# A convolution's layer norm reduced to two numbers a row, with its sums, the last tile's copy and the second projection's first chunks reordered

## The chip, the cores and the metric

One Trainium2 chip, one core of it. The metric is the device time of one execution in microseconds (us), median of several runs; a profile is one further execution, recorded instruction by instruction. PE is TensorE, PEld its weight load, DVE VectorE, ACT ScalarE, POOL GpSimd, SP the queue that issues the DMAs.

## The reference, cut to what matters

Two blocks run one after the other on 256 rows of 2048 float32 channels. The change touches the second block's convolution layer alone:

```python
u = h @ w_pw1 + b_pw1                  # 2048 -> 4096
a, gate = jnp.split(u, 2, axis=-1)
u = a * jax.nn.sigmoid(gate)
u = depthwise_conv(u, w_dw) + b_dw     # 31 taps along the rows, each channel for itself
u = silu(layer_norm_2(u, ln_g, ln_b))  # over the 2048 channels, eps 1e-5
x = x + u @ w_pw2 + b_pw2              # the second projection
```

A gated MLP of width 8192 follows.

## The kernel before, in words

Activations lie channels on partitions: a tensor is 16 tiles of 128 channels by 256 rows. All weights stream once, as 686 chunks of 128x1024 float32 (512 KB) in a fixed order written by `plan` (line 45); `STEP[c]` is chunk c. For each chunk SP issues the load (L510) into one of 7 raw slots, ACT rounds it to a high part (`high`, L623, 4 slots), DVE (L971) or POOL (L566, for the chunks in `ON_POOL`) subtracts to a low part, and PE multiplies (L1693 and L1695, or L1698 to L1700 in the convolution's first projection). `s_mm` counts chunks that PE has finished; `high(c)` needs `s_mm >= c - 3`, the load of chunk c+6 needs `s_mm >= c`. Every engine runs its instructions in the order written, in one loop over c each, so whatever waits in a loop holds all that is behind it.

Chunks 328 to 394 are the first projection, tile by tile: "a" and then "gate" ("gt"). When a gate tile t is finished (chunk 348 for t=4, 361 for 7, 374 for 10, 387 for 13, 391 for 14, 395 for 15), ACT applies tanh (L743) and DVE writes the gated product (L1089, `s_pad`). Ten tiles are convolved on DVE with 31 taps each (`taps`, L1497), six a chunk. The other six, `ON_PE` = (4, 7, 10, 13, 14, 15), go to PE: SP writes the product to DRAM (L547), waits for that, and reads it back four times shifted (L550); PE then does a "cv" chunk of 64 small matmuls (L1800). These are chunks 356, 369, 382, 395, 396 and 397. SP does the copy of tile t after the load that its gate's end allows and the next one.

The layer norm. At `PIVOT` (chunk 384) PE sums tiles 0 to 7 over the channels with a matrix of ones (L1806), ACT copies the result (L957), and DVE subtracts that provisional mean from the tiles in five groups (`centre`, L1509), ACT squares them (`conv_squares`, L864). Tiles 0 to 7 are folded in pairs (L1626, L1629). After the last cv chunk `norm_conv` of each engine finishes: PE sums values and squares as full 128x256 products, ACT and DVE work out the reciprocal root as a 128x256 tile (L1517 to L1532), and DVE and ACT then normalise two tiles at a time: subtract the mean (L1525), multiply (L1539), SiLU (L878), rounding to the high part (L881), low part (L1542).

Chunks 398 to 429 are the second projection, 16 tiles of 2 chunks. The first four tiles are interleaved: the first halves of tiles 0 to 3 (398 to 401), then the second halves. A first half needs input tiles 0 to 7. A finished tile is added to the residual (L1093, L1096; `s_comb`) and starts the next norm (L754 to L1106).

At `POST` (end of the first block) the same kind of norm is already done with two numbers a row: sums against one column of ones (`stats`, L1730), a few operations on 128x2, `across` (L1414) to spread them on a diagonal, and a product with `unit` (L1883, L1886) that gives every partition the row. Chunks 328 to 335 already serve four products each (`together`, `chunk_for_all`).

Of the kernel before, what the change touches and what calls it, by code (L numbers as in the profile page):

```python
# [8 lines left out]
F32 = mybir.dt.float32  # L9
# [6 lines left out]
T = 256  # L16
# [28 lines left out]
def plan():  # L45
# [105 lines left out]
    group(*[Job("p2", t, "W", "w_p2", t, 2) for t in range(4)])  # L151
# [41 lines left out]
ON_POOL = {c for c in range(4, 32, 2)} | set(range(P1, P1_END + 4)) - PLAIN  # L193
# [44 lines left out]
def taps_plan():  # L238
# [26 lines left out]
    for c in range(P1, P1_END + 1):  # L265
# [21 lines left out]
LN2 = P1_END  # L287

# [6 lines left out]
def _build(nc, a, out, ctx):  # L295
# [101 lines left out]
    mA, m1, m2, rs = keep  # L397
# [17 lines left out]
    def row(ap):  # L415
# [50 lines left out]
    s_piv, s_mA, s_ctr, s_lsq, s_lnm, s_m1 = (sem("s_piv"), sem("s_mA"), sem("s_ctr"), sem("s_lsq"), sem("s_lnm"),  # L466
                                              sem("s_m1"))
# [37 lines left out]
    def sync(e):  # L505
# [17 lines left out]
        for c in range(1, NC + 1):  # L523
            if c + RAW - 1 < NC:
                w.wait_ge(s_mm, c)
                chunk(c + RAW - 1)
# [15 lines left out]

            j = ended(c - 1, "gt")
            if j is not None and j.t in ON_PE:
                i = ON_PE.index(j.t)
                w.wait_ge(s_pad, ON_PE[i] + 1)
                e.dma_start(a["padded"][i, :, :], wide[i]).then_inc(s_away, 16)  # L547
                w.wait_ge(s_away, 16 * (i + 1))
                for r in range(4):
                    e.dma_start(shifted[i][32 * r:32 * r + 32, :, :], a["padded"][i, :, :].rearrange(  # L550
                        "(g c) x -> c g x", g=4)[:, :, r:r + 284]).then_inc(s_shift[i % 3], 16)
# [5 lines left out]
    def gpsimd(e):  # L557
        w = Waits(e)

        def low(c):  # L560
# [53 lines left out]
    def scalar(e):  # L614
# [27 lines left out]
        def evac(j):  # L642
# [95 lines left out]
            elif j.stage == "gt":  # L738
# [4 lines left out]
                e.activation(kept(j), of(j), ACT.Tanh, scale=0.5, bias=hb[:, t:t + 1]).then_inc(s_evac, 1)  # L743
# [5 lines left out]
            elif j.stage == "p2":  # L749
# [3 lines left out]
                w.wait_ge(s_lnm, 2)  # L753
# [112 lines left out]
        def norm_conv():  # L866
            e.preload_act_table(ACT.Sqrt)
            for n in range(2, 5):
                conv_squares(n)
            w.wait_ge(s_lnm, 1)  # L870
            e.activation(m1, bank[7][:, 0:T], ACT.Copy).then_inc(s_m1, 1)
# [1128 lines left out]
```

## Time and profile before

| | us |
|---|---|
| median of three runs | 2104.72 |
| lowest and highest | 2104.37 and 2107.44 |
| the profiled execution, its own time | 2118.45 |
| its span in the trace | 2116.7 |
| PE busy in it | 2031.1 (96%) |
| DVE, ACT and POOL busy | 1619.4, 976.7 and 405.9 |

PE is busy nearly everywhere; the profile's forty slices are 52.9 us each and only three stretches show it waiting for long: the start, 1033 to 1044 us, and 1254 to 1293 us of the span, where the convolution's norm lies. The times named below are microseconds from the span's start.

### The profile page before, as it was taken

How to read it: one execution, taken by the hardware profiler on the slowest of the kernel's cores; microseconds unless marked ns; L12 is line 12 of the kernel's file. 1: busy time of each engine (PE TensorE's matmuls, PEld its weight loads, DVE VectorE, ACT ScalarE, POOL GpSimd, SP SyncE). 2: the span in 40 equal slices, each digit the busy share in tenths (PEclk: the TensorE clock that was granted, in tenths of full speed). 3: DMA queues.
4: the chain of work that ended last, by engine and by line, in shares of the span. 5: the costliest groups of instructions: out<-in, count | busy, mean ns of one | idle time of the engine just before them, and what ended most of it. 6: DMA issues, size and time to landing. Idle time of an engine off the chain costs nothing.

```text
span 2116.7 us, 30778 instructions
## 1 busy us (share of the span) xinstructions
PE 2031.1 (96%) x12116; PEld 1753.3 (83%) x12116; DVE 1619.4 (77%) x2528; ACT 976.7 (46%) x1438; POOL 405.9 (19%) x288
## 2 busy tenths in 40 slices
PE   7999999999899999999999988999999999999997
PEld 6787887788777788888899976888888888888886
DVE  8766889989899996688899957777567657656765
ACT  5544444444444445557543335544344434434442
POOL 3400233343233320000387750000000000000000
PEclk9999999999999999999999998999999999999998
DMA  7554554444544455565456553555555555555553
GB/s 292 200 182 160 189 181 158 145 164 150 168 150 159 151 183 184 184 225 188 140 182 209 180 181 109 189 188 183 187 189 184 186 188 188 184 185 189 186 184 118
DMA packets 106704, 378.01 MB, mean 179 GB/s; under 512 B 11968, under 2 KB 15808, under 8 KB 106560
## 3 DMA queue, kind: packets, MB, share of 16 engines
q1 hardware_dynamic: 106560, 376.04, 53.2%
q8 instruction: 96, 1.57, 0.3%
q14 instruction: 48, 0.39, 0.1%
HBM read 373.01 MB, written 2.98 MB: 178 GB/s over the span
## 4 chain that ended last, share of the span: by engine, by line
PE 73%; DVE 19%; ACT 3%; issue 3%; DMA 1%; POOL 0%; SPq 0%; DVEq 0%; ACTq 0%
PE bank L1693 38%; PE bank L1695 19%; DVE wl L971 6%; PE bank L1698 2%; PE bank L1699 2%; PE bank L1700 2%; ACT wh L623 2%; PE bank L1684 1%; PE bank L1682 1%; PE bank L1683 1%; DVE scr L1002 1%; PE bank L1800 1%; DVE sq L978 1%; DVE wsc L1286 1%; DVE wm L1276 1%
## 5 line engine op out<-in xcount | busy, mean ns | idle before, releaser
L971 DVE TENSOR_TENSOR wl<-raw,wh 128x1024 fp32r<-128x1024 f32 x598 | 748.5, 1256 | 346.5 <-ACT wh L623 345.4
L623 ACT ACTIVATE wh<-raw 128x1024 fp32r<-128x1024 f32 x680 | 710.6, 1054 | 539.7 <-PE bank L1695 384.3
L1693 PE MATMUL bank<-Hr,wh 128*128 128x512 f32 x2432 | 870.4, 402 | 17.6 <-DVE wl L971 12.4
L1693 PE MATMUL bank<-Yr,wh 128*128 128x512 f32 x2240 | 801.0, 402 | 27.0 <-DVE wl L971 10.9
L1695 PE MATMUL bank<-Hr,wl 128*128 128x256 f32 x2432 | 683.7, 281 | 0.0
L1695 PE MATMUL bank<-Yr,wl 128*128 128x256 f32 x2240 | 630.7, 282 | 0.0
L1693 PEld LDWEIGHTS bank<-Hr,wh 128*128 128x128 f32 x2432 | 458.9, 189 | 141.6 <-issue 12.8
L1693 PEld LDWEIGHTS bank<-Yr,wh 128*128 128x128 f32 x2240 | 423.8, 189 | 136.3 <-DVE wl L971 11.3
L1695 PEld LDWEIGHTS bank<-Hr,wl 128*128 128x128 f32 x2432 | 461.3, 190 | 0.3
L1695 PEld LDWEIGHTS bank<-Yr,wl 128*128 128x128 f32 x2240 | 426.1, 190 | 0.2
L566 POOL TENSOR_TENSOR wl<-raw,wh 128x1024 fp32r<-128x1024 f32 x82 | 203.1, 2483 | 399.7 <-ACT wh L623 399.7
L1698 PE MATMUL bank<-Hr,wh 128*128 128x256 f32 x448 | 127.5, 285 | 1.3 <-POOL wl L566 1.2
L581 POOL TENSOR_TENSOR wcs<-tab 128x256 f32<-128x256 f32 x32 | 38.8, 1214 | 461.2 <-DVE wm L1290 319.0
L1699 PE MATMUL bank<-Hr,wh 128*128 128x256 f32 x448 | 126.8, 283 | 0.0
L1700 PE MATMUL bank<-Hr,wl 128*128 128x256 f32 x448 | 126.7, 283 | 0.0
L1497 DVE SCALAR_TENSOR_TENSOR bank<-upad,cst,bank 128x256 f32<-128x256 f32 x290 | 121.7, 482 | 2.3
L767 ACT ACTIVATE Yr<-scrB 128x256 fp32r<-128x256 f32 x64 | 26.7, 418 | 146.3 <-DVE scrB L1114 146.3
L1698 PEld LDWEIGHTS bank<-Hr,wh 128*128 128x128 f32 x448 | 85.9, 192 | 3.1 <-issue 2.7
L1699 PEld LDWEIGHTS bank<-Hr,wh 128*128 128x128 f32 x448 | 86.0, 192 | 0.0
L1700 PEld LDWEIGHTS bank<-Hr,wl 128*128 128x128 f32 x448 | 86.0, 192 | 0.0
L688 ACT ACTIVATE scr<-scr 128x256 f32<-128x256 f32 x32 | 13.4, 418 | 115.3 <-DVE scr L1002 115.3
L1117 DVE TENSOR_TENSOR Yr<-scrB,Yr 128x256 fp32r<-128x256 f32 x64 | 27.2, 425 | 31.0 <-ACT Yr L767 31.0
(307 smaller groups left out, 1754.3 us busy)
## 6 DMA issues: line engine op xcount, KB each, us to landing
raw<-in_w_up SPq DMA_DIRECT2D x128, 512.0 KB, 3.2
raw<-in_w_dn SPq DMA_DIRECT2D x128, 512.0 KB, 3.2
raw<-in_w_g SPq DMA_DIRECT2D x96, 512.0 KB, 3.3
raw<-in_w_p SPq DMA_DIRECT2D x88, 512.0 KB, 4.2
raw<-in_w_b SPq DMA_DIRECT2D x48, 512.0 KB, 3.2
raw<-in_w_out SPq DMA_DIRECT2D x32, 512.0 KB, 3.2
raw<-in_w_bx SPq DMA_DIRECT2D x16, 512.0 KB, 4.5
raw<-in_w_q SPq DMA_DIRECT2D x16, 512.0 KB, 3.3
```

Source lines behind the costliest of these rows:

```text
L566: e.tensor_tensor(wl[:, c % RAW, :], raw[:, c % RAW, :], wh[:, c % WN, :].bitcast(F32), ALU.subtract).then_inc(s_low_g, 1)
L581: e.tensor_tensor(d[:, 0, :, :], *sides(0, 0), ALU.mult)
L623: e.activation(wh[:, c % WN, :], raw[:, c % RAW, :], ACT.Copy).then_inc(s_hi, 1)
L767: e.activation(hid.hi[:, t % 16, :], kept(j), ACT.Copy).then_inc(s_hidh, 1)
L971: e.tensor_tensor(wl[:, c % RAW, :], raw[:, c % RAW, :], wh[:, c % WN, :].bitcast(F32), ALU.subtract).then_inc(s_low_v, 1)
L1117: e.tensor_tensor(hid.lo[:, t % 16, :], s, hid.hi[:, t % 16, :].bitcast(F32), ALU.subtract).then_inc(s_hidl, 1)
L1497: e.scalar_tensor_tensor(ac, pad[:, j:j + T], wj, ac, ALU.mult, ALU.add).then_inc(s_v, w.own())
L1693: e.matmul(dst.rearrange("p (h t) -> p h t", h=2), lh, pair.both[:, :, k, :], start=first_part and kk == 0, stop=last_part and kk == 7, sk ...
L1695: ins = e.matmul(dst[:, 0:T], ll, pair.hi[:, k, :], start=False, stop=last_part and kk == 7, skip_group_check=True)
L1698: e.matmul(dst[:, 0:T], lh, pair.hi[:, k, :], start=first_part and kk == 0, stop=False)
L1699: e.matmul(dst[:, 0:T], lh, pair.lo[:, k, :], start=False, stop=False)
L1700: ins = e.matmul(dst[:, 0:T], ll, pair.hi[:, k, :], start=False, stop=last_part and kk == 7)
```

## The change

1. The second projection's first four tiles become one group (`together`): each of chunks 398 to 405 holds two input tiles' weights for four products, so chunk 398 needs input tiles 0 and 1 alone. A new weight array `w_p2g` holds them in this order. POOL makes the low parts up to chunk 405 (before: 401).
2. The pivot is taken over tiles 0 to 3 at chunk 367. Centring, squares and folds are spread over other chunks; the groups are (0-3), (4-7), (8-11), (12), (13,14), (15). Tiles 8 to 11 are added to the folds.
3. PE does all sums but those of tile 15 ahead of chunk 397, tile 15's convolution, and against one column (`stats`).
4. After tile 15 the mean and the reciprocal root are worked out on 128x2 and spread by one 128x512 product; values are multiplied and then the mean's share is subtracted, tile by tile for tiles 0 and 1, then in pairs. SiLU writes to PSUM.
5. The high parts of chunks 402 to 408 are made inside ACT's `norm_conv`, each after a pair of tiles.
6. SP does the copy of a tile ahead of the load of the chunk that its gate's end allows. The gates of tiles 14 and 15 stay in PSUM.

```diff
-    group(*[Job("p2", t, "W", "w_p2", t, 2) for t in range(4)])
+    together("p2g", "w_p2g", [Job("p2", t, "W", "w_p2", 0, 8) for t in range(4)], 1, 2)
-ON_POOL = {c for c in range(4, 32, 2)} | set(range(P1, P1_END + 4)) - PLAIN
+ON_POOL = {c for c in range(4, 32, 2)} | set(range(P1, P1_END + 8)) - PLAIN
-PIVOT = end("gt", 12) + 2
+PIVOT, NEXT = end("gt", 8) + 2, end("gt", 12) + 2
-CENTRED = ((0, 4), (4, 4), (8, 4), (12, 2), (14, 2))
+CENTRED = ((0, 4), (4, 4), (8, 4), (12, 1), (13, 2), (15, 1))
+NORMED = ((0, 1), (1, 1)) + tuple((t, 2) for t in range(2, 16, 2))
+NORMED_FOR = [next(n + 1 for n, (t, nt) in enumerate(NORMED) if t <= k < t + nt) for k in range(16)]
+HIGH_LN = range(LN2 + 4, LN2 + 11)
# sync
         for c in range(1, NC + 1):
+            j = ended(c, "gt")
+            if j is not None and j.t in ON_PE:
+                i = ON_PE.index(j.t)
+                w.wait_ge(s_pad, ON_PE[i] + 1)
+                e.dma_start(a["padded"][i, :, :], wide[i]).then_inc(s_away, 16)
+                w.wait_ge(s_away, 16 * (i + 1))
+                for r in range(4):
+                    e.dma_start(shifted[i]...)
             if c + RAW - 1 < NC:
                 w.wait_ge(s_mm, c)
                 chunk(c + RAW - 1)
-            j = ended(c - 1, "gt")
...
# gpsimd, low
+            if c >= P1_END + 3:
+                w.wait_ge(s_wide, 3)
# scalar
+                if t == 15:
+                    e.preload_act_table(ACT.Sqrt)
+                    conv_squares(2)
+                    conv_squares(3)
...
         def norm_conv():
+            conv_squares(5)
             w.wait_ge(s_lneps, 1)
+            e.activation(st[:, 10:12], st[:, 10:12], ACT.Sqrt).then_inc(s_lnroot, 1)
             e.preload_act_table(ACT.Silu)
+            for n, (t0, nt) in enumerate(NORMED):
+                val = bank[4 + n % 2][:, 0:nt * T].rearrange("p (n t) -> p n t", n=nt)
+                w.wait_ge(s_lns, n + 1)
+                if n >= 2:
+                    w.wait_ge(s_cpl, n - 1)
+                for t in range(t0, t0 + nt):
+                    e.activation(val[:, t - t0, :], Mf[:, t, :], ACT.Silu, ...)
+                w.wait_ge(s_lsil, t0 + nt)
+                e.activation(cp.hi[:, t0:t0 + nt, :], val, ACT.Copy).then_inc(s_cph, 1)
+                if LN2 + 2 + n in HIGH_LN:
+                    high(LN2 + 2 + n)
-            if len(ENDED.get(c, ())) > 1:
+            if c == end("gt", 1):
                 for j in ENDED[c]:
                     evac(j)
-            if c + 3 < NC and c + 3 not in HIGH_POST:
+            if c + 3 < NC and c + 3 not in HIGH_POST and c + 3 not in HIGH_LN:
                 high(c + 3)
-            if c in (PIVOT + 2, PIVOT + 3):
-                conv_squares(c - PIVOT - 2)
+            if c in (PIVOT + 2, NEXT + 1):
+                conv_squares(0 if c == PIVOT + 2 else 1)
+            if c == LN2 - 1:
+                conv_squares(4)
# vector, gate tile 15
+                if t == 15:
+                    taps("rest")
+                    centre(2)
+                    centre(3)
+                    w.wait_ge(s_ctr, 3)
+                    w.wait_ge(s_fold, 1)
+                    e.tensor_tensor(fold[0], fold[0], Mf[:, 8:12, :], ALU.add).then_inc(s_fold, 1)
+                    w.wait_ge(s_evac, j.evac)
+                e.scalar_tensor_tensor(pad[:, 15:271], of(j) if t >= 14 else kept(j), 1.0, ...)
+                if t == 15:
+                    w.wait_ge(s_lsq, 3)
+                    w.wait_ge(s_fold, 2)
+                    e.tensor_tensor(fold[1], fold[1], F1[:, 8:12, :], ALU.add).then_inc(s_fold, 1)
# vector, norm_conv
+            centre(5)
+            w.wait_ge(s_lnm, 1)
+            e.tensor_scalar(st[:, 14:18], bank[7][:, 0:4], 1.0, None, ALU.mult).then_inc(s_v, w.own())
+            e.tensor_tensor(mm, m, m, ALU.mult)
+            e.scalar_tensor_tensor(rs, sq, 1e-5, mm, ALU.add, ALU.subtract).then_inc(s_lneps, 1)
+            e.reciprocal(rs, rs)
+            e.tensor_tensor(mr, m, rs, ALU.mult)
+            e.tensor_tensor(dg, ident..., st[:, 10:14]..., ALU.mult).then_inc(s_dg, 1)
+            times(0)
+            for n, (t0, nt) in enumerate(NORMED):
+                f = Mf[:, t0:t0 + nt, :]
+                e.tensor_tensor(f, f, row(bank[6][:, T:2 * T]).broadcast_to((128, nt, T)), ALU.subtract)
+                if n + 1 < len(NORMED):
+                    times(n + 1)
+                if n >= 1:
+                    low_part(n - 1)
+            low_part(len(NORMED) - 1)
# vector, main loop
-            if c in (PIVOT + 1, PIVOT + 2):
-                centre(c - PIVOT - 1)
-            if c == PIVOT + 4:
+            if c in (PIVOT + 1, NEXT):
+                centre(0 if c == PIVOT + 1 else 1)
+            if c == LN2 - 1:
+                centre(4)
+            if c == NEXT + 2:
                 ... fold[0] of tiles 0 to 7
-            if c == PIVOT + 5:
+            if c == NEXT + 3:
                 ... fold[1]
# tensor
             if c == PIVOT:
-                conv_done(w, range(8))
-                sum_of(7, Mf, range(8), first_part=True, last_part=True).then_inc(s_piv, 1)
+                conv_done(w, range(4))
+                sum_of(7, Mf, range(4), first_part=True, last_part=True).then_inc(s_piv, 1)
+            if c == LN2 - 1:
+                sums_conv()
             if c == LN2:
                 norm_conv()
```

PE's `sums_conv` waits for the folds and then runs `stats` over fold[0] (4 tiles), fold[1] (4), tiles 12, 13 and 14 and their squares; its `norm_conv` runs `stats` over tile 15 and its squares, waits for `dg` and does the product `unit` by `dg`, 128x512.

## Rows read from the trace of the kernel before

**Rows 1.** The page's costliest groups: the three that make a chunk's two parts.

```profile
L971 DVE TENSOR_TENSOR wl<-raw,wh 128x1024 fp32r<-128x1024 f32 x598 | 748.5, 1256 | 346.5 <-ACT wh L623 345.4
L623 ACT ACTIVATE wh<-raw 128x1024 fp32r<-128x1024 f32 x680 | 710.6, 1054 | 539.7 <-PE bank L1695 384.3
L566 POOL TENSOR_TENSOR wl<-raw,wh 128x1024 fp32r<-128x1024 f32 x82 | 203.1, 2483 | 399.7 <-ACT wh L623 399.7
```

**Rows 2.** Table of stretches: PE, PEld, DVE, ACT, POOL busy, granted clock, DMA.

```profile
1254.40:1260.30 5.90, 0.05 (x6) 0.06 (x5) 0.78 (x1) 1.42 (x2) 2.57 (x2) 0.90 0.66 181
...
1262.00:1264.00 2.00, 2.00 (x24) 1.07 (x20) 0.00 (x0) 0.00 (x0) 0.00 (x0) 0.50 0.00 0
...
1289.00:1291.00 2.00, 1.74 (x6) 1.46 (x6) 1.97 (x3) 1.19 (x3) 0.00 (x0) 0.50 0.04 8
...
1295.00:1297.00 2.00, 2.00 (x13) 1.75 (x12) 1.02 (x2) 1.97 (x4) 0.00 (x0) 1.00 0.56 147
```

**Rows 3.** Timeline of PE (start, duration, instruction, idle before and releaser).

```profile
1210.09 3.62 PE L1806 MATMUL bank<-Mf,ones 128*128 128x256 f32 x16
...
1234.71 0.36 PE L1698 MATMUL bank<-Hr,wh 128*128 128x256 f32 x1 [0.85 <-POOL wl L566]
...
1247.30 7.11 PE L1800 MATMUL bank<-shifted,raw 128*32 128x256 f32 x128
1260.27 6.42 PE L1800 MATMUL bank<-shifted,raw 128*32 128x256 f32 x64 [5.85 <-DMA shifted<-padded]
...
1275.08 1.03 PE L1806 MATMUL bank<-F,ones 128*128 128x256 f32 x4
1283.21 0.77 PE L1693 MATMUL bank<-Yr,wh 128*128 128x512 f32 x1 [7.11 <-DVE Yr L1542]
...
1293.31 0.40 PE L1693 MATMUL bank<-Yr,wh 128*128 128x512 f32 x1
...
1293.66 0.39 PE L1693 MATMUL bank<-Yr,wh 128*128 128x512 f32 x1
```

**Rows 4.** Timeline of DVE from tile 12's product to the folds.

```profile
1208.56 2.55 DVE L1089 SCALAR_TENSOR_TENSOR upad<-scrB,scrB 128x256 f32<-128x256 f32 x1
...
1229.97 0.41 DVE L1089 SCALAR_TENSOR_TENSOR wide<-scrB,scrB 128x256 f32<-128x256 f32 x1
...
1234.37 1.27 DVE L1626 TENSOR_TENSOR fold<-Mf 128x1024 f32<-128x1024 f32 x1
1235.57 3.41 DVE L1629 TENSOR_TENSOR fold<-F 128x1024 f32<-128x1024 f32 x1
```

**Rows 5.** Timeline of SP's queue: tile 13's copy and the loads behind it.

```profile
1230.41 0.33 SPq L547 DMA_DIRECT2D padded<-wide  x1
1232.16 1.76 SPq L550 DMA_DIRECT2D shifted<-padded  x4
1233.96 1.38 SPq L510 DMA_DIRECT2D raw<-in_w_cv  x3
```

**Rows 6.** DMA view, 1190.3 to 1190.9: a load behind tile 10's copy, us to landing.

```profile
raw<-in_w_cv SPq DMA_DIRECT2D x1, 512.0 KB, 4.8
```

**Rows 7.** Timelines of ACT and DVE inside the norm.

```profile
1268.25 1.28 ACT L867 ACT_TABLE_LOAD   x1
...
1280.59 1.09 ACT L878 ACTIVATE Mf<-Mf,cst 128x256 f32<-128x256 f32 x2 [1.25 <-DVE Mf L1539]
1281.71 0.63 ACT L881 ACTIVATE Yr<-Mf 128x512 fp32r<-128x512 f32 x1
...
1282.37 0.69 DVE L1542 TENSOR_TENSOR Yr<-Mf,Yr 128x512 fp32r<-128x512 f32 x1
```

**Rows 8.** Timeline of PE at POST: sums against one column, and the spreading product.

```profile
1036.14 1.03 PE L1730 MATMUL bank<-ones,scrB 128*128 128x1 f32 x8
...
1040.02 1.19 PE L1883 MATMUL bank<-dg,unit 128*128 128x256 f32 x2 [1.31 <-DVE dg L1414]
```

**Rows 9.** Timeline of DVE: the second projection's first tile is added.

```profile
1305.51 0.48 DVE L1093 SCALAR_TENSOR_TENSOR Xf<-bank,cst,Xf 128x256 f32<-128x256 f32 x1
```

More of the change, by code:

```diff
@@ L263, in batch @@
                 return
-    for c in range(P1, P1_END + 1):
+    for c in range(P1, end("gt", 15)):
         for j in ENDED.get(c, ()):
@@ L396, in _build @@
     st = small[:, 32:64]
-    mA, m1, m2, rs = keep
+    mA = keep[0]
     def cv(name, i=0):
@@ L1511, in norm_conv @@
         def norm_conv():
-            taps("rest")
-            centre(2)
-            centre(3)
-            centre(4)
-            w.wait_ge(s_m1, 1)
-            e.tensor_tensor(m2, m1, m1, ALU.mult).then_inc(s_v, w.own())
-            n = w.n
-            def less(t0):
-                f = Mf[:, t0:t0 + 4, :]
-                w.wait_ge(s_ctr, 5)
-                w.wait_ge(s_lsq, 5)
-                w.wait_ge(s_fold, 1)
-                e.tensor_tensor(f, f, row(m1).broadcast_to((128, 4, T)), ALU.subtract).then_inc(s_v, w.own())
@@ L1527, in norm_conv @@
[L1527 to L1543 removed]
+            m, sq = st[:, 14:16], st[:, 16:18]
@@ new lines, in norm_conv, with times @@
+            w.wait_ge(s_v, w.n)
+            e.tensor_tensor(mr, m, rs, ALU.mult).then_inc(s_v, w.own())
+            w.wait_ge(s_v, w.n)
+            e.tensor_tensor(dg, ident[:, None, :].broadcast_to((128, 4, 128)),
+                            st[:, 10:14][:, :, None].broadcast_to((128, 4, 128)), ALU.mult).then_inc(s_dg, 1)
+            def times(n):
+                t0, nt = NORMED[n]
+                f = Mf[:, t0:t0 + nt, :]
+                w.wait_ge(s_wide, 3)
+                w.wait_ge(s_ctr, 6)
+                w.wait_ge(s_lsq, 6)
+                e.tensor_tensor(f, f, row(bank[6][:, 0:T]).broadcast_to((128, nt, T)),
+                                ALU.mult).then_inc(s_v, w.own())
@@ L1719, in chunk_for_all @@
                     a, z = k == 0 and j.col == 0, k == 15
+                    if j.kind == "W":
+                        both = bank[j.banks[0]]
+                        e.matmul(both.rearrange("p (h t) -> p h t", h=2), lh, pair.both[:, :, k, :], start=a, stop=z,
+                                 skip_group_check=True)
+                        ins = e.matmul(both[:, 0:T], ll, pair.hi[:, k, :], start=False, stop=z, skip_group_check=True)
+                        if z and j.tells:
+                            ins.then_inc(s_grp, 1)
+                        continue
                     e.matmul(of(j), lh, pair.hi[:, k, :], start=a, stop=False, skip_group_check=True)
@@ L1808, in sum_of, with sums_conv @@
             return ins
[L1810 to L1826 removed]
+        def sums_conv():
+            w.wait_ge(s_mA, 1)
+            w.wait_ge(s_fold, 4)
+            for t in range(4):
+                stats(fold[0][:, t, :], 0, first_part=t == 0)
+            for t in range(4):
+                stats(fold[1][:, t, :], 2)
+            w.wait_ge(s_ctr, 4)
+            stats(Mf[:, 12, :], 0)
+            w.wait_ge(s_lsq, 4)
+            stats(F1[:, 12, :], 2)
+            w.wait_ge(s_ctr, 5)
+            for t in (13, 14):
+                stats(Mf[:, t, :], 0)
+            w.wait_ge(s_lsq, 5)
+            for t in (13, 14):
+                stats(F1[:, t, :], 2)
+        def norm_conv():
+            w.wait_ge(s_ctr, 6)
+            stats(Mf[:, 15, :], 0)
+            w.wait_ge(s_lsq, 6)
+            stats(F1[:, 15, :], 2).then_inc(s_lnm, 1)
+            w.wait_ge(s_dg, 3)
+            e.matmul(bank[6], unit, dg, start=True, stop=True).then_inc(s_wide, 1)
         for c in range(NC):
```

103 lines of the change are left out of this document (37 added, 66 removed).

## Prediction

> **What bounds the kernel now.** I read the page first: PE is busy for 96% of the span, so time can only come from the stretches where it waits or runs at the lower of its two clocks, 1.2 and 2.4 GHz. The table of stretches then shows where: from 1254.4 to 1260.3 PE does nothing, after that the granted clock is 0.50 (1.2 GHz), and it is 0.50 again in the second projection's first chunks, where PE is busy 1.74 of 2 us [rows 2]. The timeline of PE gives the waits: 5.85 us for tile 15's copy, then tile 15's convolution in 6.42 us where two such chunks had taken 7.11 together, then sums until 1276.1, then 7.11 us in which DVE and ACT work out the norm [rows 3]. One sum over eight tiles, the pivot, stands in the middle of weight chunks (1210.1 to about 1213.4), and behind it PE waits 0.85 us for POOL's low part [rows 3]. Last I read what limits the helpers around chunk 387: DVE's timeline [rows 4] and SP's queue [rows 5].
>
> Two marks measure the change: E, the end of tile 15's convolution (1266.7 before [rows 3]), and N, the time at which chunk 406 can start. Before, PE reaches the higher clock at 1293.31 with 12 of the group's 64 weight tiles multiplied, and one takes 0.35 us (1293.31 to 1293.66) [rows 3]: 52 x 0.3475 = 18.1, so N = 1311.4, or E + 44.7. Behind N PE runs through in both kernels.
>
> **Part 1, from N backwards: the norm and the grouped chunks.** After E, ACT first makes chunk 401's high part (1.05, [rows 1]) and evacuates tile 15 (about 0.5); DVE's centring, no longer beside a POOL part, and the square take about 0.45 each (by the 0.48 of a tile-wide operation [rows 9]); the last four records of the sums half of 1.03 [rows 8]; with the handovers 3.3. At POST, PE stands 1.31 us between its last sum and the spreading product [rows 8]; here there are three more small operations (0.2 each, an estimate) and `dg` is twice as wide (+0.3): 2.2. The product has 512 columns for 256: 1.19 at the lower clock [rows 8], taken twice without its fixed part, 2.1 (at the higher clock about 1.2). So the row stands in PSUM at E + 7.6. Before, PE's first product of the projection began at 1283.2, E + 16.5 [rows 3].
>
> Of the normalisation DVE does six operations ahead of the first low part's end, four of them and the low part itself a tile wide and one two tiles (0.69 [rows 7]): 3.0. Chunk 398 needs just two tiles, 8 x 0.64 = 5.1 us at the lower clock, and ends at 8.2 after the row. Then the order on ACT decides: `high(402)` to `high(408)` each wait until PE has finished the chunk four before, and the next SiLU stands behind it. From the end of a chunk: high part 1.05 [rows 1], SiLU of two tiles 1.09, its high part 0.63, DVE's low part 0.69 [rows 7], handovers 0.15: 3.6, then the chunk that this feeds, 2.8: two chunks in 6.4, or 3.2 for one, where PE needs 2.8. Chunk 400 ends at 13.8, 402 at 20.1, 404 at 26.5, 405 at 29.3.
>
> A wait comes in behind it: chunk 406 writes the bank of the group's first product and needs `s_comb`. All four products end with chunk 405. DVE's loop does `low(409)` ahead of that evacuation, and ACT can't make its high part before chunk 405 is done: 1.05 + 1.26 [rows 1] + two operations of 0.48 [rows 9], 3.4 in all. The evacuations of the four (some 2.5 each) stand in front of `low(410)`; that is 14 us for which four chunks of 2.8 and the 3.4 are the cover: just enough. N = E + 7.6 + 29.3 + 3.4 = E + 40.3. **Part 1 gains 4.4.**
>
> **Part 2, up to E.** The pivot falls from 16 records to 8 (3.3 us, [rows 3]): -1.6. Its place, and `conv_squares` moved away from chunks 386 and 387, also take away the idle time behind it: 1213.4 to 1247.3 for eleven chunks of 2.88 leaves 2.2. So without a new wait chunk 393 would start at 1238.
>
> The new wait is SP's. Tile t's copy now stands ahead of the load of chunk e+6, where e is the chunk count at its gate's end. SP waits for the product, writes (1.75 until the next issue), issues four reads (1.8) [rows 5], and only then the load, which takes 4.8 beside them [rows 6]; ACT 1.05 and POOL 2.48 [rows 1] follow: 12.0 from the product to the chunk's readiness. PE wants it 6 x 2.88 = 17.3 after the gate's end. So the product must be there 5.3 after it. For tiles 4, 7 and 10 it is there after 3.9: cover 1.4, cost nothing on PE; but ACT stands 4 to 5 us in the high part of the waiting chunk, the next gate's tanh is some 2 us late, and DVE, full since chunk 367, keeps part of that.
>
> For tile 13 the product is late already before: it starts at 1229.97 [rows 4], 7.6 after the gate's end (1213.4 + 3 x 2.9 = 1222.3). Now: tile 12's product starts at about 1211.0 (1208.6 [rows 4], plus the first centring moved ahead of it, 2.6, and ACT's lateness, less the idle time that swallows a part). From it to tile 13's there were 21.4 us with two centrings of 2.65; now one, which POOL no longer blocks (1.2), and the first fold, moved ahead (1.27 alone, 3.4 beside POOL [rows 4]; I take 2.0): 21.4 - 5.3 + 3.2 = 19.3. It starts at 1230.3, and if POOL's low part comes first, as it did between the two folds, it is done at 1232.7; the ends are 1227 (nothing late at tile 11, fold at 1.2) and 1233. The gate's end is now at 1220.6. Chunk 393 is ready at 1232.7 + 12.0 = 1244.7 instead of 1238: **PE waits 6.7**, bounds 1 and 7.
>
> From there PE is full: chunks 393 and 394 2 x 2.88; the clock lost in the wait, 1.5 (bounds: 0, and 2.9 for one chunk at half rate); two convolution chunks 7.1 [rows 3]; the sums ahead of chunk 397, 56 records at 0.115 = 6.4 [rows 8], and 0.2 of waiting; tile 15's convolution 3.6 at the higher clock, since no idle time stands ahead of it: E = 1244.7 + 24.6 = 1269.3. Under the sums are hidden tile 15's copy (product at 1256.4, which itself waits for `high(398)` on ACT, then 7.1 for write and reads and landing to 1263.6, sums until 1265.7) and tile 14's centring. **Part 2 costs 2.6**; bounds -5.6 and +4.
>
> The squares of tiles 8 to 12 now follow a table load set behind tile 15's tanh. In the trace the load takes 1.28 and the next ACTIVATE starts 1.3 after it [rows 7]; squares, fold and sums start at 1259.6, just when PE is ready. By the Trainium skill (ScalarE: Activation LUTs, What ACT_TABLE_LOAD costs) a switch of set costs about 2.66 us with its drain. The trace doesn't agree; by the page E would be 1.4 later.
>
> **Sum.** +2.6 - 4.4 = -1.8, against the profiled execution's span of 2116.7 (own time 2118.45, 0.65% above the median; I carry the difference over as it is): 2104.72 - 1.8 = 2102.9. About 0.2% (4.2 us) is what a measurement can tell from no change.
>
> **Rivals.** (a) Chunk 393 waits little or not at all: the product comes before 1228, because DVE catches up or a late chunk delays PE and not DVE. Then E = 1238 + 23.1 = 1261.1, -5.6, and the whole is -10.0: 2094.7; with half the wait 2099. For it: PE has a large cover in every other copy. Against: DVE's own line leaves it no idle time from 1208 on [rows 4].
>
> (b) The grouped chunks stay at the lower clock: PE waits 0.4 in each 3.2, and before it was at 0.50 while busy 1.74 of 2 [rows 2]. Five more chunks at 5.1 for 3.2 would cost 9.5; but at 5.1 PE is busy throughout, as it was when it rose at 1293, so one or two chunks, 2 to 4 us: -1.8 + 4 = +2, 2107. By the Trainium skill (TensorE: Matmul & The Clock Gate, A second HAM failure mode) short idle times between groups of matmuls can make the clock go up and down.
>
> (c) Slower: the wait at chunk 393 drops the clock, and it stays at 1.2 GHz through 393, 394 and both convolution chunks, as it stayed over all of tile 15's (6.42 us at 0.50, [rows 2, 3]). That is 2.9 + 2.9 + 2.8 + 2.8 = 11.4 instead of 1.5: +9.9, 2112.8. It decides once three of the four are slow (+6 or more on -1.8). Against: weight chunks brought the clock back at 1293 within four microseconds of full work.
>
> (d) It does nothing: both halves hide behind the copy of tile 15. Then the time is 2104.7. Against: the 16.5 us after E lie in nobody's shade.
>
> **Chances.** Forecast 0.50 (own range 2099.5 to 2105.5), (a) 0.25, (b) 0.12, (c) 0.09, (d) 0.04. Faster than 2100.5: most of (a) and a quarter of the forecast, 0.36. Slower than 2108.9: (c) and a little of (b), 0.11. The rest 0.53. The range 2096 to 2108 leaves out the lower half of (a) and (c).
>
> **What would show it.** In the timeline of PE: the pivot with 8 records near 1159; a wait of about 6.7 us before chunk 393 near 1238, with the load issued about 1236 behind tile 13's reads; sums of 128x1 ahead of tile 15's convolution and that in 3.6 us; PE's first projection product 10 to 11 us after E; chunks 400 to 405 each 3.2 apart; a wait of some 3.4 us ahead of chunk 406 for DVE's L1096 operation. No wait at chunk 393 makes the forecast wrong toward (a); a clock of 0.50 behind it for over 6 us, toward (c).

## The result and the profile of the changed kernel

| | before | changed |
|---|---|---|
| median of nine runs, us | 2104.72 | 2113.36 |
| lowest and highest, us | 2103.35 and 2110.36 | 2110.08 and 2125.55 |
| the profiled execution, its own time | 2118.45 | 2117.75 |
| its span | 2116.7 | 2116.0 |

The ratio is 1.0039, 95% interval 1.0028 to 1.0051: about 8.2 us slower, clearly more than a measurement needs. Forecast were 2102.9 and a range of 2096 to 2108. The prediction was wrong, in its sign as well.

The two spans are nearly alike and must not be compared as wholes. PE ran through the second block's MLP in 100 us stretches of 568 records in the one profile and of 579 in the other, 2% apart, in a part that the change leaves alone; what causes it is not known. So I measure on PE between two marks that bracket the change: from the first product of the first projection to the product that starts the MLP's norm. From the timeline of PE, before and after:

```profile
1044.52 0.55 PE L1720 MATMUL bank<-Hr,wh 128*128 128x256 f32 x1 [1.75 <-issue]
...
1386.21 0.38 PE L1736 MATMUL bank<-keep,ones 128*128 128x256 f32 x1
```

```profile
1048.81 0.55 PE L1772 MATMUL bank<-Hr,wh 128*128 128x256 f32 x1 [1.75 <-issue]
...
1399.00 0.59 PE L1788 MATMUL bank<-keep,ones 128*128 128x256 f32 x2
```

That is 341.7 and 350.2: 8.5 us more, about what the medians say (8.6). The changed kernel's profile runs 4.3 us late from its first mark on, so 4.3 is to be taken from its times when they are set beside those of before.

The changed kernel's timeline of PE through the region answers to [rows 3] and [rows 8]:

```profile
1164.04 1.89 PE L1858 MATMUL bank<-Mf,ones 128*128 128x256 f32 x8
...
1248.65 0.55 PE L1742 MATMUL bank<-Hr,wh 128*128 128x256 f32 x1 [5.91 <-POOL wl L570]
...
1264.02 3.73 PE L1782 MATMUL bank<-ones,fold 128*128 128x1 f32 x32
1267.62 0.85 PE L1782 MATMUL bank<-ones,Mf 128*128 128x1 f32 x4
1268.33 0.99 PE L1782 MATMUL bank<-ones,F 128*128 128x1 f32 x4
1269.19 1.85 PE L1782 MATMUL bank<-ones,Mf 128*128 128x1 f32 x8
1270.89 1.84 PE L1782 MATMUL bank<-ones,F 128*128 128x1 f32 x8
1272.67 6.28 PE L1852 MATMUL bank<-shifted,raw 128*32 128x256 f32 x64
1281.01 0.66 PE L1782 MATMUL bank<-ones,Mf 128*128 128x1 f32 x4 [2.07 <-DVE Mf L1534]
...
1284.53 2.08 PE L1887 MATMUL bank<-dg,unit 128*128 128x512 f32 x2 [2.00 <-DVE dg L1552]
1289.33 0.77 PE L1766 MATMUL bank<-Yr,wh 128*128 128x512 f32 x1 [2.73 <-POOL wl L570]
...
1321.05 0.51 PE L1737 MATMUL bank<-Yr,wh 128*128 128x512 f32 x1 [3.31 <-DVE Xf L1121]
```

Four things are to be seen. The wait ahead of chunk 393 is there, 5.91 us. The one-column sums begin at 0.117 us a record (3.73 for 32) and end at 0.23 (1.84 for 8), with no idle time between. Tile 15's convolution, with no wait ahead of it, still takes 6.28. And the wait of 3.31 stands ahead of chunk 406. (The releaser at 1289.33 is misread: POOL's low part had begun at 1286.75 for a later chunk; DVE's first low part of the norm ended at 1289.24.)

The table of stretches of the changed kernel (columns as in [rows 2]) shows what the sums do to the granted clock:

```profile
1257.00:1264.00 7.00, 7.00 (x129) 4.04 (x128) 1.65 (x2) 5.35 (x7) 3.48 (x2) 1.00 0.57 200
1264.00:1267.60 3.60, 3.60 (x36) 3.58 (x33) 1.86 (x1) 1.42 (x2) 3.53 (x2) 1.00 1.03 291
1267.60:1272.70 5.10, 5.10 (x30) 5.08 (x30) 0.65 (x1) 0.63 (x1) 0.10 (x1) 0.52 0.35 142
1272.70:1279.00 6.30, 6.25 (x65) 2.77 (x64) 0.00 (x0) 0.00 (x0) 0.00 (x0) 0.58 0.00 0
...
1322.00:1326.00 4.00, 4.00 (x16) 3.38 (x15) 2.78 (x9) 1.43 (x4) 0.00 (x0) 0.57 0.00 0
```

PE's records are back to back from 1257 to 1279, yet the granted clock is 0.52 (1.2 GHz) from 1267.6 to 1272.7 and 0.58 from there to 1279. The load on the memory doesn't explain it: DMA was at 1.03 in the stretch with the clock at 1.00, and at 0.00 in the last of these with 0.58. The last line is the wait ahead of chunk 406 at work: behind it ten records run at the lower clock.

DVE's and SP's timelines of the changed kernel answer to [rows 4] and [rows 5]: the fold and the slowed product of tile 13, then the write, the reads, and only then the two weight loads.

```profile
1232.41 1.90 DVE L1666 TENSOR_TENSOR fold<-Mf 128x1024 f32<-128x1024 f32 x1
1234.23 2.62 DVE L1110 SCALAR_TENSOR_TENSOR wide<-scrB,scrB 128x256 f32<-128x256 f32 x1
```

```profile
1236.88 0.33 SPq L531 DMA_DIRECT2D padded<-wide  x1
1238.63 1.75 SPq L534 DMA_DIRECT2D shifted<-padded  x4
1240.43 0.91 SPq L513 DMA_DIRECT2D raw<-in_w_p  x2
```

### The profile page after: what moved, and what is told of

It is laid out like the page before. It is cut to its first block, busy times and chain, and to the rows that moved or that the text cites. A ratio compares the mean times of both kernels' runs of the same rounds, so it can differ in the third digit from the quotient of the medians.

```text
span 2116.0 us, 30837 instructions
## 1 busy us (share of the span) xinstructions
PE 2027.8 (96%) x12134; PEld 1756.1 (83%) x12134; DVE 1606.3 (76%) x2537; ACT 976.9 (46%) x1439; POOL 413.0 (20%) x292
## 4 chain that ended last, share of the span: by engine, by line
PE 69%; DVE 22%; issue 3%; ACT 3%; DMA 2%; SPq 1%; POOL 0%; ACTq 0%; DVEq 0%; POOLq 0%
PE bank L1737 38%; PE bank L1739 19%; DVE wl L983 7%; DVE bank L1522 2%; ACT wh L627 2%; PE bank L1726 1%; PE bank L1728 1%; PE bank L1727 1%; PE bank L1742 1%; PE bank L1743 1%; PE bank L1744 1%; DVE scr L1014 1%; PE bank L1852 1%; DMA raw<-in_w_p 1%; DVE wm L1301 1%
## 5 line engine op out<-in xcount | busy, mean ns | idle before, releaser
L1737 PE MATMUL bank<-Yr,wh 128*128 128x512 f32 x2176 | 770.4, 399 | 23.6 <-DVE wl L983 11.4
L1739 PE MATMUL bank<-Yr,wl 128*128 128x256 f32 x2176 | 609.0, 280 | 0.0
L1737 PEld LDWEIGHTS bank<-Yr,wh 128*128 128x128 f32 x2176 | 410.8, 189 | 125.4 <-DVE wl L983 11.8
L1739 PEld LDWEIGHTS bank<-Yr,wl 128*128 128x128 f32 x2176 | 412.0, 189 | 0.2
L570 POOL TENSOR_TENSOR wl<-raw,wh 128x1024 fp32r<-128x1024 f32 x86 | 213.0, 2486 | 424.3 <-ACT wh L627 405.2
```

The lines of the kernel that those rows point to most:

```text
L1737: e.matmul(dst.rearrange("p (h t) -> p h t", h=2), lh, pair.both[:, :, k, :], start=first_part and kk == 0, stop=last_part and kk == 7, sk ...
L1739: ins = e.matmul(dst[:, 0:T], ll, pair.hi[:, k, :], start=False, stop=last_part and kk == 7, skip_group_check=True)
```

## The experiments

The theory after reading the two traces has three costs: the wait at chunk 393; the clock that falls within the one-column sums and slows them and tile 15's convolution; the wait ahead of chunk 406 and the clock behind it. Each is tried alone against the changed kernel, then all together. "Ratio" is against the kernel before, "on PE" the time between the two marks (341.7 before, 350.2 changed). The second column scatters by some 1.5 us: the part behind chunk 406 took 77.9 us in some profiles and 76.6 in others with the same instructions, a weight tile every 0.353 us in the former and every 0.347 in the latter; the clock came back up to 2 us sooner or later in the group; and the wait at chunk 393 was anything from 5.45 to 7.09 us in the six profiles whose kernels leave the copies and the folds as the changed kernel has them.

| kernel | ratio (95% interval) | on PE |
|---|---|---|
| changed kernel | 1.0039 (1.0028 to 1.0051) | 350.2 |
| 1 all copies late | 1.0008 (0.9991 to 1.0024) | 342.8 |
| 2 two tiles' sums behind | 1.0018 (1.0007 to 1.0029) | 347.5 |
| 3 bank 7 | 1.0018 (1.0008 to 1.0029) | 349.7 |
| 4 wide products beside the sums | 1.0038 (1.0026 to 1.005) | 349.2 |
| 5 chunk 401's high part later | 1.0033 (1.001 to 1.0057) | 345.9 |
| 6 tile 13's copy alone late | 1.0031 (1.0013 to 1.0048) | 346.3 |
| 7 bank 7, evacuations spread | 1.0013 (0.9999 to 1.0027) | 345.9 |
| 8 all together | 0.9967 (0.9954 to 0.998) | 338.3 |
| 9 and tile 15's gate first | 0.9973 (0.9964 to 0.9982) | 336.1 |
| 10 folds behind tile 13's product | 1.0023 (1.0012 to 1.0034) | 344.4 |
| 11 as 9, with POOL's low parts | 0.9964 (0.995 to 0.9977) | 335.0 |
| 12 as 11, tile 15's copy early | 0.9953 (0.9934 to 0.9973) | 334.5 |

### 1. All copies where they were

```diff
-            j = ended(c, "gt")
-            if j is not None and j.t in ON_PE:
...
             if c + RAW - 1 < NC:
                 w.wait_ge(s_mm, c)
                 chunk(c + RAW - 1)
+            j = ended(c - 1, "gt")
+            if j is not None and j.t in ON_PE:
...
```

> SP does every tile's copy where the kernel before did it, behind the load of the next chunk; all else as in the changed kernel. Theory (the wait of 5.9 us at chunk 393 is the load held behind tile 13's copy, and the slow stretch behind it belongs to it; tile 15's copy keeps a cover of 8.7 us of sums): no wait at chunk 393, about 1.1 us less at the lower clock, tile 15's copy 1.4 us later but still covered: 7 us less than the changed kernel, 2106.4; the granted clock still falls in the one-column sums and tile 15's convolution still takes 6.3 us. Rival (the time is lost at tile 15 anyway): PE waits the same 6 us before tile 15's convolution and the time stays at 2113. Second rival (the wait at chunk 393 is what lowers the clock later): tile 15's convolution takes 3.6 us and the time is 2104 or less.

Measured: 6.5 us of the 8.2 come back by the ratios, 7.4 on PE. No wait at chunk 393; the clock falls in the sums all the same (0.95 from 1256 to 1260, 0.50 from 1260) and tile 15's convolution still runs mostly at the lower clock. So both rivals fall, and the wait at chunk 393, with the clock lost behind it, is the largest cost of the change. But the old order turns out to have a cost of its own. SP's timeline of this kernel, from tile 14's write on:

```profile
1242.35 0.33 SPq L534 DMA_DIRECT2D padded<-wide  x1
1247.82 1.75 SPq L537 DMA_DIRECT2D shifted<-padded  x4
1249.61 1.85 SPq L513 DMA_DIRECT2D raw<-in_w_p2g  x4
1251.51 0.93 SPq L534 DMA_DIRECT2D padded<-wide  x1
1260.81 1.75 SPq L537 DMA_DIRECT2D shifted<-padded  x4
```

Tile 14's write took 5.5 us until its reads could be issued and tile 15's 9.3, each behind four weight loads just issued; tile 13's, with no load just issued, 1.75. PE waits 1.84 for tile 14's reads here and 0.55 for tile 15's. Putting the copy ahead of the loads shortens the write; it only mustn't be done for a tile whose product is late.

### 2. The sums of tiles 13 and 14 behind tile 15's convolution

```diff
             stats(F1[:, 12, :], 2)
+
+        def norm_conv():
             w.wait_ge(s_ctr, 5)
             for t in (13, 14):
                 stats(Mf[:, t, :], 0)
             w.wait_ge(s_lsq, 5)
             for t in (13, 14):
                 stats(F1[:, t, :], 2)
-
-        def norm_conv():
             w.wait_ge(s_ctr, 6)
             stats(Mf[:, 15, :], 0)
```

> The sums of tiles 13 and 14 (16 records, 3.5 us at the lower clock) stand behind tile 15's convolution instead of ahead of it. Theory: tile 15's convolution starts 3.5 us earlier (about 1269.2), provided its reads have landed, and the sums then fill the 2.1 us in which PE waits for tile 15's centring, and stick out of it by 1.6 at the lower clock, 0 at the higher: 1.9 to 3.5 us less than the changed kernel, 2110 to 2111.5. The granted clock falls at the same point of the sums (1267.6), since 44 such records stand ahead of it. Rival (the copy of tile 15 lands only when the sums end): PE waits 3 us for the reads and nothing is gained, 2113 to 2115.

Measured: 2.7 on PE, 4.4 by the ratios (whose intervals overlap). The convolution followed the sums without a wait (its reads had landed), and took 6.12; so 40 one-column records ahead of it cost the clock as 56 did. Behind it the clock had risen, the 16 records took 2.0, and PE waited only 0.19 for tile 15's centring. A gain as forecast, from work that fits into a wait. From the timeline of PE:

```profile
1265.27 6.12 PE L1852 MATMUL bank<-shifted,raw 128*32 128x256 f32 x64
1271.31 1.05 PE L1782 MATMUL bank<-ones,Mf 128*128 128x1 f32 x8
```

### 3. Chunk 406 in a free bank

```diff
+        if t == 4:
+            j = jobs[-1]
+            held[j.banks[0]] = j.before[0]
+            b, j.banks, j.before = j.banks[0], [7], []
```

> The fifth tile of the second projection (chunks 406 and 407) goes to bank 7, which is free, instead of bank 0, which waits for the group's first evacuation. Theory: the wait of 3.3 us ahead of chunk 406 goes and with it the 1.8 us at the lower clock behind it: 5.1 less than the changed kernel, 2108.3. Rival (the wait only moves: the four evacuations stand ahead of the low part of chunk 410, and PE waits there): PE waits 2 to 3 us before chunk 410 and the time is 2111 to 2113.

Measured: 0.5 on PE, 4.4 by the ratios, whose intervals just overlap. In this profile the wait at chunk 393 was 7.09, and tile 15's convolution ended 1.0 us later than in the changed kernel; behind it 1.5 us were gained, not 5.1. The trace bears out the rival: the 3.31 is gone, and PE waits ahead of chunk 410, four chunks further on, behind the four evacuations on DVE, with the clock down again for ten records:

```profile
1327.61 0.47 PE L1741 MATMUL bank<-Yr,wh 128*128 128x512 f32 x1 [1.77 <-DVE wl L987]
```

The prediction had said of this cover "just enough"; with the wait of 3.4 it was, without it it isn't.

### 4. Wide products beside the one-column sums

This kernel adds 14 products whose results nobody reads.

```diff
+        def both(src, col, first_part=False):
+            stats(src, col, first_part)
+            e.matmul(bank[6][:, 0:T], ones, src, start=True, stop=True)
...
-                stats(fold[0][:, t, :], 0, first_part=t == 0)
+                both(fold[0][:, t, :], 0, first_part=t == 0)
```

(and so for all 14 pairs)

> Each pair of one-column sums ahead of tile 15's convolution has a product of 128x256 with the same tile behind it, whose result nobody reads: 14 of them, 0.43 us each at the higher clock, 6.0 us of added work. Theory (records of one column let the granted clock fall, however busy PE is): the clock stays at 1.00, the sums take 6.4 + 6.0 = 12.4 us for 8.7, tile 15's convolution 3.6 for 6.3: +1.0, 2114.4, and the norm's product of 128x512 takes up to 0.9 less. Rival (the clock falls for another cause, the wait at chunk 393 or the load on the memory): it falls all the same, tile 15's convolution takes 6.3 us, and the time is 2119 or more.

The table of stretches and the timeline of PE of this kernel:

```profile
1262.00:1274.00 12.00, 12.00 (x83) 11.33 (x84) 0.72 (x1) 2.05 (x3) 4.55 (x2) 1.00 0.48 159
1274.00:1278.00 4.00, 4.00 (x66) 2.04 (x65) 0.00 (x0) 0.00 (x0) 0.00 (x0) 1.00 0.02 4
```

```profile
1274.39 3.66 PE L1852 MATMUL bank<-shifted,raw 128*32 128x256 f32 x64
```

The clock stays at 1.00, the sums and the added products take 12.5 us for 8.7, the convolution 3.66 for 6.28, and the time is that of the changed kernel (1.0038) though PE has 6 us more to do. The wait at chunk 393 (5.45) was there too, so it isn't what lowers the clock at tile 15. A row made of one-column records alone is. The Trainium skill (TensorE: Matmul & The Clock Gate, The HAM clock gate) says that the gate goes by how busy PE has been lately; here records without a gap let it fall, so busy time as the profile counts it doesn't decide.

### 5. Chunk 401's high part off the path

```diff
             e.preload_act_table(ACT.Silu)
+            high(LN2 + 3)
             for n, (t0, nt) in enumerate(NORMED):
```

> ACT makes chunk 401's high part (1.06 us) behind tile 15's squares, the square root and the table load instead of ahead of tile 15's evacuation. Theory (it stands on the path from tile 15's convolution to the norm, and its new place is idle): PE waits 1.0 us less for tile 15's centring (1.1 for 2.07) and nothing is late behind it: 1.0 less than the changed kernel. Rival (chunk 401's low part then comes later than PE wants it, or the first SiLU is late): the microsecond comes back before chunk 401 and the time stays.

Measured: PE waits 1.06 for the centring instead of 2.07, and nothing is late behind it. The rest of the 4.3 on PE is mostly the scatter named above (1.0 in the group, 1.4 behind chunk 406); the ratio can't tell one microsecond.

### 6. Tile 13's copy alone late

```diff
-            if j is not None and j.t in ON_PE:
+            if j is not None and j.t != 13 and j.t in ON_PE:
...
                 chunk(c + RAW - 1)
+            j = ended(c - 1, "gt")
+            if j is not None and j.t == 13:
...
```

> Only tile 13's copy stands behind the next load; the others stay ahead. In the kernel with all copies late, tile 14's write took 5.1 us to land and tile 15's 9 us, behind three to four weight loads, where in the changed kernel they took 1.8. Theory: no wait at chunk 393, no wait for tile 14's reads (1.84 with all late) nor for tile 15's (0.55): 8 to 9.5 us less than the changed kernel on PE, measured up to the FFN's first chunks, about 2 less than with all copies late. The granted clock still falls in the one-column sums and tile 15's convolution takes 6 us. Rival (the queue to the memory is full in any order): the 1.84 stays, and the kernel is as fast as with all copies late.

A miss. Chunk 393 doesn't wait and tile 14's reads are in time, but PE waits elsewhere, and between the marks the kernel takes 3.5 us more than with all copies late (the intervals of the ratios overlap). Its timelines of PE and ACT:

```profile
1255.67 2.05 PE L1791 MATMUL bank<-ones,fold 128*128 128x1 f32 x9 [4.59 <-DVE fold L1124]
```

```profile
1250.51 1.06 ACT L636 ACTIVATE wh<-raw 128x1024 fp32r<-128x1024 f32 x1 [11.72 <-DMA raw<-in_w_p2g]
1251.47 0.43 ACT L756 ACTIVATE bank<-bank,small 128x256 f32<-128x256 f32 x1
1251.92 1.28 ACT L759 ACT_TABLE_LOAD   x1
```

ACT stands in chunk 398's high part, whose load SP holds behind tile 14's copy. Behind it are tile 15's tanh and the squares for the second fold. In the changed kernel ACT had stood in the same place for 9.67 us, but PE, delayed at chunk 393, came later than the fold: a wait that was covered by another wait.

### 7. The group's evacuations, one a chunk

```diff
+_c = AT["p2", 0].end
+for _t, _at in ((1, _c + 1), (2, _c + 2), (3, _c + 3), (4, _c + 3)):
+    _j = AT["p2", _t]
+    ENDED[_j.end].remove(_j)
+    ENDED.setdefault(_at, []).append(_j)
```

(on top of experiment 3)

> As the kernel with bank 7, and the evacuations of the group's four tiles are spread over the loops of four chunks (one each) instead of all standing ahead of chunk 410's low part. With bank 7 alone the wait of 3.3 before chunk 406 became one of 1.77 before chunk 410, the clock fell there too, and only 0.7 of 5.1 us was gained on PE up to the FFN. Theory: no wait in chunks 406 to 412 and the clock stays at 1.00: 5 us less than the changed kernel on PE. Rival (DVE has too much to do in these chunks in any order: 3.4 us of evacuation and low part a chunk for 2.8): a wait of 1 to 2 us comes at a later chunk and the gain is under 2.

Measured: 4.3 on PE, 5.5 by the ratios. Between the two: no wait in chunks 406 to 412 and no fall of the clock there, but DVE needs 3.9 us for an evacuation and a low part where PE takes 2.8 for a chunk, and two waits of 0.95 and 0.90 come some chunks later.

### 8. All together

Experiments 2, 5, 6 and 7, and the first fold's sums between the convolutions of tiles 13 and 14:

```diff
+            if c == LN2 - 2:
+                w.wait_ge(s_mA, 1)
+                w.wait_ge(s_fold, 3)
+                for t in range(4):
+                    stats(fold[0][:, t, :], 0, first_part=t == 0)
```

> All together: only tile 13's copy late, chunk 401's high part behind the squares, bank 7 and the spread evacuations, the sums of tiles 13 and 14 behind tile 15's convolution, and the first fold's sums (16 records) between the convolution chunks of tiles 13 and 14, so that only 20 or so one-column records stand in a row ahead of tile 15's. Theory (the costs add up, and a row of one-column records shorter than the 3.6 us after which the clock fell leaves it at 1.00): 8.5 for the copy, 2.5 for the sums, 2.6 for the convolution at the higher clock, 1.0, and 5 behind the group: 18 to 20 less than the changed kernel, 2093 to 2095, which is 10 faster than the kernel before. Rival (the clock falls all the same, since a row of 2.8 us is enough): 3 us less of gain, 2097. Second rival (without the waits PE meets tile 15's reads before they have landed): a wait of 2 to 4 us before tile 15's convolution.

Measured: 12 less than the changed kernel on PE and 15 by the ratios; 7 us faster than the kernel before. Less than the 18 to 20 expected, by a wait of 2.96 for the second fold (experiment 6's chain on ACT) and the fallen clock: the convolution took 6.6. With that wait ahead of the sums, this kernel can't tell whether a short row leaves the clock alone; experiment 12 comes nearer.

```profile
1260.89 0.99 PE L1801 MATMUL bank<-ones,Mf 128*128 128x1 f32 x4
1261.74 0.99 PE L1801 MATMUL bank<-ones,F 128*128 128x1 f32 x4
1262.66 6.59 PE L1871 MATMUL bank<-shifted,raw 128*32 128x256 f32 x64
```

### 9. Tile 15's gate ahead of chunk 398's high part

```diff
-            if c == end("gt", 1):
+            if c in (end("gt", 1), end("gt", 15)):
                 for j in ENDED[c]:
                     evac(j)
             if c + 3 < NC and c + 3 not in HIGH_POST and c + 3 not in HIGH_LN:
                 high(c + 3)
```

(on top of 8)

> All together, and on ACT the gate of tile 15 ahead of chunk 398's high part. With all together PE waited 2.96 us ahead of the one-column sums for the second fold, whose squares stood behind tile 15's tanh on ACT, and that behind chunk 398's high part, whose load SP held behind the copies: the tanh came 8 us after PE's end of the gate (1245.8 to 1253.8). Theory: the tanh now comes at once, the product, squares and fold about 8 us earlier, tile 15's write 6 us earlier (it stands behind more loads in flight), PE does not wait ahead of the sums, and tile 15's convolution starts 3 to 4 us earlier; if the clock stays at 1.00 it takes 3.6 us for 6.6: 3 to 7 less than all together, 2093 to 2097. Rival (the write of tile 15 now takes as long as with all copies late, 9 us, behind four loads): tile 15's reads land as late as before, PE waits for them ahead of its convolution, and the time stays within 1 us of all together.

Measured: the same by the ratios, 2.2 less on PE. The tanh comes at once (1246.30), the wait for the fold is gone, and the rival takes its place: tile 15's write is issued at 1249.59, its reads only at 1256.77, and PE waits 3.66 for them.

### 10. The folds behind tile 13's product

```diff
-            if c == NEXT + 2:
+            if c == NEXT + 4:
                 w.wait_ge(s_ctr, 2)
...
-            if c == NEXT + 3:
+            if c == NEXT + 5:
                 w.wait_ge(s_lsq, 2)
```

(in the changed kernel)

> The changed kernel with both first folds two chunks later on DVE, behind tile 13's product. Theory (SP's hold of chunk 393's load lasts until tile 13's product, and that is late because DVE has the fold and the centring ahead of it): the product starts 1.9 us earlier and, if POOL is not beside it, takes 0.65 for 2.6: the wait at chunk 393 falls from 5.9 to between 2 and 4 us, and the whole by as much. Rival (DVE is behind for another reason, the taps): the product does not come earlier and the wait stays at 6.

The product takes 1.10 for 2.62 and the wait falls from 5.91 to 2.96. By the ratios the kernel gains 3.4, on PE 5.8. DVE's and PE's timelines:

```profile
1225.41 1.10 DVE L1110 SCALAR_TENSOR_TENSOR wide<-scrB,scrB 128x256 f32<-128x256 f32 x1
```

```profile
1238.72 0.36 PE L1742 MATMUL bank<-Hr,wh 128*128 128x256 f32 x1 [2.96 <-POOL wl L570]
```

So the fold ahead of it accounts for half of the wait at chunk 393, and removing that half gains 3.0 of wait and 0.9 at the lower clock behind it. The other 1.4 of the 5.8 lies behind chunk 406 and is the scatter named above.

### 11 and 12. POOL's low parts up to chunk 409; tile 15's copy ahead of chunk 398's load

```diff
-ON_POOL = {c for c in range(4, 32, 2)} | set(range(P1, P1_END + 8)) - PLAIN
+ON_POOL = {c for c in range(4, 32, 2)} | set(range(P1, P1_END + 12)) - PLAIN
```

> As the kernel with the gate first, and POOL makes the low parts of chunks 406 to 409 too. With the evacuations spread, DVE needed 3.9 us for each evacuation and low part where PE takes 2.8 for a chunk, and PE waited 0.6 to 0.95 us twice some chunks later. Theory: DVE has the evacuations alone, PE waits for no low part, 1 to 2 us less than with the gate first. Rival (POOL's 2.4 us beside DVE makes DVE's operations longer, as it did in the fold of 1.2 that took 1.9 and the product of 0.65 that took 2.6): no gain, or 1 us more.

Measured: 1.1 less on PE than experiment 9, one wait of 0.96 left of two. The intervals overlap.

```diff
-            j = ended(c, "gt")
+            j = AT["gt", 15] if c == end("gt", 15) - 3 else ended(c, "gt") if c < end("gt", 15) else None
```

> As the kernel with POOL's low parts, and SP does tile 15's copy ahead of the loads of chunks 398 to 400, which PE wants only after the norm. There tile 15's write took 7.2 us behind those loads (1249.6 to 1256.8 with the gate first), PE waited 2.8 to 3.7 us for tile 15's reads, and the granted clock fell in that wait, so that its convolution took 4.9 to 5.3 us instead of 3.6, though it had stayed at 1.00 through 24 one-column records. Theory (the write waits in the memory queues behind the loads): it takes 1.8 us, no wait ahead of tile 15's convolution, the clock stays at 1.00 and the convolution takes 3.6: 4 to 5 us less, 2093 to 2094. Rival (chunks 398 to 400 are then loaded so late that their high parts on ACT hold up the evacuations of tiles 13 and 14 and with them the sums behind tile 15's convolution): PE waits 1 to 3 us behind it, the clock falls there, and the gain is 0 to 2.

A miss in size; the timeline of PE:

```profile
1253.80 1.95 PE L1801 MATMUL bank<-ones,fold 128*128 128x1 f32 x16
1255.60 0.58 PE L1801 MATMUL bank<-ones,Mf 128*128 128x1 f32 x4
1256.05 0.58 PE L1801 MATMUL bank<-ones,F 128*128 128x1 f32 x4
1256.96 5.35 PE L1871 MATMUL bank<-shifted,raw 128*32 128x256 f32 x64 [0.32 <-DMA shifted<-padded]
1264.27 0.27 PE L1801 MATMUL bank<-ones,Mf 128*128 128x1 f32 x1 [1.96 <-DVE Mf L1553]
```

The table of stretches:

```profile
1253.80:1256.60 2.80, 2.80 (x28) 2.75 (x24) 0.00 (x0) 0.00 (x0) 0.00 (x0) 1.00 0.81 220
1258.00:1260.00 2.00, 2.00 (x24) 1.31 (x20) 0.00 (x0) 1.18 (x2) 1.02 (x1) 0.50 1.00 395
```

The wait for the reads is 0.32 for 2.79, but the write still took 4.8 us, behind tile 14's reads and one weight load, the high parts of chunks 398 to 400 now hold up the evacuations (the rival; PE waits 1.96 and then 0.54 for centrings), and the convolution takes 5.35. Through 24 one-column records the clock stays at 1.00; behind them and a wait of 0.32 it is 0.50. Waits of 0.6 among the grouped chunks had left it at 1.00, so the short row has its part in the fall, and experiment 8's hope that such a row leaves the clock alone did not hold here. What the row and the 0.32 do each by itself was not separated. 0.9953 is the best ratio of the study, 10 us faster than the kernel before, but not told apart from experiments 8 and 11.

## Why the prediction was wrong

By its own steps, in us:

| step | forecast | measured |
|---|---|---|
| pivot | 8 records near 1159 | 8, at 1164.0 less 4.3 |
| start of tile 13's product | 1230.3 | 1234.2 less 4.3 |
| wait at chunk 393 | 6.7 | 5.9 |
| chunks 393 and 394 with the lost clock | 7.3 | 8.3 |
| sums ahead of tile 15's convolution | 6.6 | 8.7 |
| tile 15's convolution | 3.6 | 6.3 |
| E against before | +2.6 | +8.0 |
| E to the row in PSUM | 7.6 | 7.7 |
| row to the end of chunk 398 | 8.2 | 8.3 |
| end of 398 to the end of 405 | 21.1 | 22.9 |
| wait ahead of chunk 406 | 3.4 | 3.3 |
| E to N | 40.3 | 42.1 |
| clock lost behind N | 0 | 1.7 |

**The step that failed** is in part 2: "tile 15's convolution 3.6 at the higher clock, since no idle time stands ahead of it", with the sums at "56 records at 0.115" throughout. I took idle time to be the only thing that lowers the clock. The rows at hand showed one-column sums at the higher rate, 1.03 for eight [rows 8], and I read their duration there and not what comes behind them. The trace of the kernel before had it to be read, in the records right behind those eight and in the table of stretches (here PE, the granted clock, and DMA alone):

```profile
1037.72 0.99 PE L1730 MATMUL bank<-ones,extra 128*128 128x1 f32 x4
```

```profile
1034.80:1037.20 2.40, 2.13 (x18) 1.00 0.42 167
1037.20:1038.70 1.50, 1.50 (x8) 0.51 0.00 0
```

The clock falls at 1037.2, in the middle of one-column records without a gap, 2.4 us after a wait of 1.28 and 1.4 after one of 0.24, and four of them take 0.99. Experiment 4, in which the clock stays up with a wide product behind each pair of sums, shows the cause: 2.1 in the sums and 2.7 in the convolution, 4.8 of the 5.4 by which E was missed. With them the sum would have been -1.8 + 4.8 = +3.0, on the other side of no change; the clock behind chunk 393 (1.1 more), the group's pace (1.8) and the clock behind N (1.7), less 0.8 of wait, make it 6.8.

**The wait at chunk 393 was right**, in place, mechanism and size, and so was its cause (experiments 1 and 10). It was the dearest part of the change, and it was in the sum. The clock behind it was 1.1 dearer than taken, within its bound of 2.9: 25 records ran slow.

**Part 1 was right in mechanism and too high in size**: 2.6 gained for 4.4. The grouped chunks 400 to 405 came 6.6 us a pair, each pair behind a wait of 0.6; I had taken 5.6 for the first two chunks behind 398 and 6.4 a pair behind them. Two of part 1's own terms don't come out of its rows: 1.05 + 1.26 + 0.96 is 3.3, not 3.4, and the "14 us" of evacuations is 10 by its own 2.5 each; with the low part between them experiment 7 shows 3.9 each, 15.6 for four. "Behind N PE runs through" was wrong by 1.7: the clock was lower for ten records behind the wait of 3.3 us, as it was for 25 behind the one of 5.9.

**The rivals.** (c) has the right time, 2112.8, and the wrong place: the clock came back within 6 us behind chunk 393, and both convolution chunks of tiles 13 and 14 ran at 7.1 together. It was down at tile 15, where (c) didn't look. (a) didn't happen, since the product was as late as forecast. (b) didn't: in the group the clock stayed at 1.00 with waits of 0.6. The range of 2096 to 2108 bounded the clock only at chunk 393, so that it missed even what a mild form of (c) would give.

The sum against the marks: 8.0 up to E, -2.6 from E to N (N of before worked out, not read), +1.7 of clock behind N, +1.4 of scatter there, is 8.5. What remains open is why a row of 24 one-column records followed by a wait of 0.3 went with a fall of the clock, as a row of 56 did. A row of 16, as between the two convolutions in experiments 8, 9, 11 and 12, left it at 1.00, but was seen in that one place only. Folding the sums into wide products with the same results was not tried.

## What to carry to other kernels

Look at what a matrix engine's records do, and not only at whether they leave gaps: a long row of products of one column (here 24 records and more) counts as busy in the profile and still cost the work behind it the clock, so put such a row where the engine would wait anyway, and not ahead of wide work. A copy moved ahead of a load in one queue helps where its source is early and holds the load where its source is late; decide it tile by tile, from the time at which the source is ready. And when a wait is taken away, look at which queue it had been covering: three of these experiments moved a wait rather than removed it.

## What the runs showed of the hardware

- The granted clock fell to 1.2 GHz within back-to-back records of one column, 3.6 us into the row in the changed kernel, and stayed at 1.00 when every four of them had a product of 256 columns (two records) behind them.
- A write of 144 KB took 1.75 us until its reads could be issued when no load had just been issued, 5.5 behind four weight loads of 512 KB and 9.3 behind four others with reads in flight (experiment 1).
- DVE's product of 128x256 from two SBUF tensors took 2.62 us beside POOL's low parts, 1.10 in experiment 10, where POOL was busy too, 0.41 in the kernel before, where POOL was idle [rows 4], and 0.42 for tile 14, with one input in PSUM and POOL busy. The Trainium skill (GPSIMD Engine Reference, Specifications) says that POOL shares its SBUF interfaces with VectorE, and that instructions with two SBUF inputs contend; the trace agrees.
